# Where the block sums of x lie in SBUF: pads of 64 and 192 bytes around their low parts instead of 64 and 64

## The chip, the core and the metric

The kernel runs on one core of a Trainium2 chip. The metric is device time in microseconds from start to end of one execution, as a median of several runs.

## The reference

Two layers of a hybrid model on one sequence of 512 tokens with 1024 features, all in fp32. Each layer is a half-weighted SwiGLU feed-forward, a mixer (a gated linear recurrence with block attention in the first layer, a convolution branch with indexed attention in the second) and a second feed-forward:

```python
def swiglu(x, w_gate, w_up, w_down):
    return (jax.nn.silu(x @ w_gate) * (x @ w_up)) @ w_down

for i in range(DEPTH):                       # DEPTH = 2
    h = rms_norm(x, ffn1_norm[i])
    x = x + 0.5 * swiglu(h, ffn1_w_gate[i], ffn1_w_up[i], ffn1_w_down[i])   # 1024 -> 2816 -> 1024
    h = rms_norm(x, mix_norm[i])
    x = x + (even_mixer if i % 2 == 0 else odd_mixer)(h, ...)
    h = rms_norm(x, ffn2_norm[i])
    x = x + 0.5 * swiglu(h, ffn2_w_gate[i], ffn2_w_up[i], ffn2_w_down[i])
return x
```

## The kernel before

**Precision.** Every product is made of three fp32r matmuls: each operand is split into a high part (ScalarE, a copy that rounds) and a low part (VectorE, the value minus its high part), and high times high, high times low and low times high are added in PSUM. The three stand in `product` (lines 814 to 816, 512 columns in most uses) and in `gu_product` (lines 877 to 879, 256 columns). Each matmul loads its own 128x128 weights. In the profile's names, `ps_y<-xu_lo,gw_hi` is the matmul that streams `xu_lo` past the weights `gw_hi`: the moving operand stands first.

**The feed-forward.** There are four, each with 22 hidden tiles of 128 rows. The first two of each are plain: x (`xs_hi`, `xs_lo`) is streamed with 512 columns past gate and up weights. For the other twenty, 80 in all, gate and up are computed together by a scheme that saves one block product of eight: it needs sums of x's blocks and sums of weight blocks. Seven calls of `gu_product` make one tile, each with four triples, so 12 matmuls of 256 columns. Four calls stream blocks of x itself (`of_u`, from `xs_hi` and `xs_lo`), three stream the block sums (`of_xu`, from `xu_hi` and `xu_lo`). In a tile's steady order they are x, x, sums, x (the one left over from the tile before), sums, sums, x. After tiles 6, 14 and 22 come eight down units each, in which the hidden values `a_hi`, `a_lo` are streamed with 512 columns past `w_hi`, `w_lo`. All of this is issued in an order written out by hand; engines are tied by semaphores. Weights come by DMA into `raw` (down and mixer weights) and `gu` (gate and up weights), and ScalarE and VectorE split them into `w_hi`, `w_lo`, `gw_hi`, `gw_lo`. The block sums are written only at the start of each feed-forward: four ScalarE copies (line 1381) and four VectorE subtractions (line 1920).

**The mixers** use the same region of SBUF as the block sums for tiles of their own (`xc`, `isc`, `c_pad1` to `c_pad3`, `cv`, `ki`, `probs_more` and others), and the region of `gu`, `gw_hi`, `gw_lo` for q, k, v and the turned probabilities `pt`.

**Addresses.** `sb` gives each tile the next free bytes of a partition, rounded up to 32, from `top[0]`. `HALF_LINE` (64) is added to `top[0]` before and behind `xu_lo`. The first tile, `xu_hi`, lies at byte 1152. By the sizes of the tiles these are the offsets of their first bytes modulo 256; steps within the tiles that a matmul reads (blocks, pieces, halves of 256 columns) are multiples of 256, except in the convolutions, which stream `a` at steps of one element:

| tiles | before | after |
|---|---|---|
| `xu_hi` | 128 | 128 |
| `xu_lo` | 192 | 192 |
| mixers' tiles below the pads: `xc_hi`, `xc_lo` / `ki_hi`, `ki_lo`, `probs_more` | 128 / 0 | 128 / 0 |
| `xt`, `xs_hi`, `xs_lo`, `raw`, `w_hi`, `w_lo`, `a_hi`, `a_lo`, `scr` | 0 | 128 |
| `ident`, `ones` | 128 | 0 |
| `t0`, `t1`, `t2`, `diag`, `sqb`, `acc`, `rstd`, `half`, `bias_t` | 192 | 64 |
| `gu`, `gw_hi`, `gw_lo`; `q`, `k`, `v`, `pt`, `probs`, `bdr_hi` in the mixers | 64 | 192 |

And the distances, moving operand minus weights, modulo 256:

| pair | before | after |
|---|---|---|
| `xs_hi`, `xs_lo` past `gw_hi`, `gw_lo` | 192 | 192 |
| `xs`, `a` past `w`; `pt` past `v`; `k` past `q` | 0 | 0 |
| `xu_hi` past `gw_hi`, `gw_lo` | 64 | 192 |
| `xu_lo` past `gw_hi` | 128 | 0 |

```python
def gu_product(ps, piece, hi, lo, first, wait=None):
    for j in range(PAIRS):                   # 4
        ...
        pe.matmul(ps, gw_hi[:, piece, w], hi(j), ...)      # line 877
        pe.matmul(ps, gw_hi[:, piece, w], lo(j), ...)      # line 878
        mm = pe.matmul(ps, gw_lo[:, piece, w], hi(j), ...) # line 879
```

Of the kernel before, what the change touches and what calls it, by code (L numbers as in the profile page):

```python
# [49 lines left out]
SKEW = 640  # L50
COPIES = 32
HALF_LINE = 64

FFN_UNITS = len(GROUPS) * KT
PAIRS = KT // 2
# [137 lines left out]
def build(nc, xt_in, gu_stream, w_stream, vec_in, bd_in, relb_in, onehot_in, ident_in, out):  # L193
# [3 lines left out]
    with ExitStack() as ctx:  # L197
        top = [(nc.sbuf_base + 31) // 32 * 32]

        def sb(name, shape, dt=F32, at=None):  # L200

            size = int(np.prod(shape[1:])) * 4
            if at is None:
                at, top[0] = top[0], top[0] + (size + 31) // 32 * 32
            return nc.alloc_sbuf_tensor_at(name, shape, dt, offset=at)
# [6 lines left out]
        xu_hi = sb("xu_hi", [P, PAIRS, 3 * TH], F32R)  # L212
        top[0] += HALF_LINE
        xu_lo = sb("xu_lo", [P, PAIRS, 3 * TH], F32R)
        top[0] += HALF_LINE
        low_top = top[0]
        xt = sb("xt", [P, KT * T])
        xs_hi = sb("xs_hi", [P, KT, T], F32R)
# [2604 lines left out]
```

## Time and profile before

| | |
|---|---|
| median of 3 runs | 1905.33 us (1904.15 to 1905.38) |
| the profiled execution | 1904.64 us, its span 1902.8 us |
| granted TensorE clock over the span | 0.998 |
| TensorE busy | 1872.6 us (98%), 11916 matmuls |
| VectorE / ScalarE / GpSimd busy | 1458.7 / 1021.4 / 194.8 us |
| DMA moved | 271.66 MB, mean 143 GB/s |

A matmul's busy time in the groups is a latency with a modelled end, and neighbours overlap: the pace at which matmuls follow each other is the distance of their starts in the timeline, which prints them in hundredths of a microsecond. Twelve matmuls of 256 columns, one `gu_product`, are long enough to read a pace to 1 ns a matmul.

### The profile page before, as it was taken

What the parts mean: (1) busy time and instruction counts of PE and PEld (TensorE: products, weight loads), DVE (VectorE), ACT (ScalarE), POOL (GpSimd) and SP (SyncE); (2) the same over time, 40 slices, a digit from 0 to 9 for tenths busy, and PEclk for the clock granted to TensorE, in tenths of its full rate; (3) what the DMA queues carried; (4) which work ended last, traced back from release to release, by engine and by line L of the source; (5) the groups of instructions that cost most, each with busy time, mean ns of one, the idle gap of its engine ahead of it and who ended that gap; (6) DMA issues with size and microseconds to landing.
All of it is one profiled execution on the core that took longest, in us unless ns stands there. A gap on an engine that the chain in (4) does not pass through costs nothing.

```text
span 1902.8 us, 31445 instructions
## 1 busy us (share of the span) xinstructions
PE 1872.6 (98%) x11916; PEld 1668.0 (88%) x11916; DVE 1458.7 (77%) x2330; ACT 1021.4 (54%) x1640; POOL 194.8 (10%) x251
## 2 busy tenths in 40 slices
PE   7999999999999999999999999999999999999999
PEld 6899899888779899998889989887778789899997
DVE  8879587577679788597877859756989878687684
ACT  7546264477776355364645526455456766364451
POOL 1311010000001011010011101011111001011010
PEclk9999999999999999999999999999999999999999
DMA  7666662211137565563465546166765376565441
GB/s 241 155 200 183 174 167 64 100 67 67 56 111 183 167 169 146 150 173 109 134 170 156 152 143 179 45 165 161 167 153 131 86 200 170 158 183 161 133 112 67
DMA packets 94789, 271.66 MB, mean 143 GB/s; under 512 B 10504, under 2 KB 10760, under 8 KB 94640
## 3 DMA queue, kind: packets, MB, share of 16 engines
q1 hardware_dynamic: 63456, 201.22, 30.7%
q0 software_dynamic: 29232, 64.50, 19.3%
q10 hardware_dynamic: 1952, 3.93, 1.1%
q8 instruction: 95, 1.56, 0.3%
q14 instruction: 54, 0.44, 0.1%
HBM read 223.07 MB, written 2.77 MB: 119 GB/s over the span
## 4 chain that ended last, share of the span: by engine, by line
PE 88%; DVE 7%; ACT 3%; issue 2%; DMA 0%; DVEq 0%; ACTq 0%
PE ps_unit L814 13%; PE ps_unit L815 13%; PE ps_unit L816 13%; PE ps_y L878 6%; PE ps_y L877 6%; PE ps_y L879 6%; PE ps_s L877 4%; PE ps_s L878 4%; PE ps_t L878 4%; PE ps_t L877 4%; PE ps_t L879 4%; PE ps_s L879 4%; PE ps_s L814 1%; DVE cv L2479 1%; PE ps_s L815 1%
## 5 line engine op out<-in xcount | busy, mean ns | idle before, releaser
L1423 ACT ACTIVATE gw_hi<-gu 128x512 fp32r<-128x512 f32 (+1 forms) x400 | 319.0, 799 | 151.5 <-PE ps_s L879 69.3
L1954 DVE TENSOR_TENSOR gw_lo<-gu,gw_hi 128x512 fp32r<-128x512 f32 (+1 forms) x400 | 354.6, 901 | 46.5 <-ACT gw_hi L1423 35.0
L814 PE MATMUL ps_unit<-a_hi,w_hi 128*128 128x512 f32 x892 | 351.0, 394 | 5.4 <-DVE w_lo L1885 2.8
L815 PE MATMUL ps_unit<-a_lo,w_hi 128*128 128x512 f32 x892 | 348.0, 390 | 0.0
L816 PE MATMUL ps_unit<-a_hi,w_lo 128*128 128x512 f32 x845 | 329.2, 390 | 0.0
L1358 ACT ACTIVATE w_hi<-raw 128x1024 fp32r<-128x1024 f32 (+1 forms) x125 | 125.3, 1003 | 305.1 <-PE ps_unit L816 301.4
L814 PEld LDWEIGHTS ps_unit<-a_hi,w_hi 128*128 128x128 f32 x892 | 167.6, 188 | 44.3 <-DVE w_lo L1885 5.1
L2091 DVE TENSOR_TENSOR t<-ps_unit,half 128x512 f32<-128x512 f32 x96 | 66.4, 691 | 172.8 <-PE ps_unit L816 172.4
L815 PEld LDWEIGHTS ps_unit<-a_lo,w_hi 128*128 128x128 f32 x892 | 167.6, 188 | 32.8
L816 PEld LDWEIGHTS ps_unit<-a_hi,w_lo 128*128 128x128 f32 x845 | 158.6, 188 | 33.8
L879 PE MATMUL ps_y<-xu_hi,gw_lo 128*128 128x256 f32 x640 | 180.5, 282 | 0.0
L878 PE MATMUL ps_y<-xu_lo,gw_hi 128*128 128x256 f32 x640 | 179.2, 280 | 0.0
L877 PE MATMUL ps_y<-xu_hi,gw_hi 128*128 128x256 f32 x640 | 178.6, 279 | 0.0
L1885 DVE TENSOR_TENSOR w_lo<-raw,w_hi 128x1024 fp32r<-128x1024 f32 (+1 forms) x125 | 143.8, 1151 | 12.9 <-ACT w_hi L1358 12.9
L759 POOL DMA_DIRECT2D gu<-gu_stream_dram x80 | 74.8, 936 | 712.5 <-DMA gu<-gu_stream_dram 698.9
L814 PE MATMUL ps_unit<-xs_hi,w_hi 128*128 128x512 f32 x360 | 145.2, 403 | 0.0
L815 PE MATMUL ps_unit<-xs_lo,w_hi 128*128 128x512 f32 x360 | 140.6, 391 | 0.0
L877 PE MATMUL ps_s<-xs_hi,gw_hi 128*128 128x256 f32 x480 | 133.3, 278 | 0.0
L878 PE MATMUL ps_s<-xs_lo,gw_hi 128*128 128x256 f32 x480 | 133.3, 278 | 0.0
L878 PE MATMUL ps_t<-xs_lo,gw_hi 128*128 128x256 f32 x480 | 133.3, 278 | 0.0
L879 PE MATMUL ps_s<-xs_hi,gw_lo 128*128 128x256 f32 x480 | 133.2, 277 | 0.0
L877 PE MATMUL ps_t<-xs_hi,gw_hi 128*128 128x256 f32 x480 | 133.2, 277 | 0.0
(324 smaller groups left out, 4648.7 us busy)
## 6 DMA issues: line engine op xcount, KB each, us to landing
gu<-gu_stream_dram SPq DMA_DIRECT2D x176, 512.0 KB, 5.1
raw<-w_stream_dram SPq DMA_DIRECT2D x136, 512.0 KB, 3.3
gu<-gu_stream_dram SPq DMA_DIRECT2D x80, 256.0 KB, 3.0
gu<-gu_stream_dram POOLq DMA_DIRECT2D x80, 256.0 KB, 4.0
gu<-gu POOLq DMA_DIRECT2D x80, 256.0 KB, 3.3
w_lo<-raw POOLq DMA_DIRECT2D x28, 512.0 KB, 4.9
raw<-w_stream_dram SPq DMA_DIRECT2D x32, 384.0 KB, 3.5
w_lo_3rd<-raw POOLq DMA_DIRECT2D x15, 512.0 KB, 4.7
```

The lines of the kernel that those rows point to most:

```text
L759: pool.dma_start(gu[:, 8 + r, :], gu_stream[f, 1][:, 1, :], accum_op=ALU.add).then_inc(s1_landed, 16)
L814: pe.matmul(ps, lhs_hi, rhs_hi, start=first, stop=False)
L815: pe.matmul(ps, lhs_hi, rhs_lo, start=False, stop=False)
L816: return pe.matmul(ps, lhs_lo, rhs_hi, start=False, stop=last)
L877: pe.matmul(ps, gw_hi[:, piece, w], hi(j), start=first and j == 0, stop=False, skip_group_check=True)
L878: pe.matmul(ps, gw_hi[:, piece, w], lo(j), start=False, stop=False, skip_group_check=True)
L879: mm = pe.matmul(ps, gw_lo[:, piece, w], hi(j), start=False, stop=j == PAIRS - 1, skip_group_check=True)
L1358: act.activation(w_hi[:, s, 0:width(n)], raw[:, slot, 0:width(n)], ACT.Copy).then_inc(w_hi_done, 1)
L1423: act.activation(gw_hi[:, w, :], src, ACT.Copy).then_inc(gw_hi_done, 1)
L1885: dve.tensor_tensor(w_lo[:, s, w], raw[:, slot, w], w_hi[:, s, w].bitcast(F32), ALU.subtract).then_inc(w_lo_done, 1)
L1954: dve.tensor_tensor(gw_lo[:, w, :], src, gw_hi[:, w, :].bitcast(F32), ALU.subtract).then_inc(gw_lo_done, 1)
L2091: dve.tensor_tensor(t0[:, :], ps_unit[:, s, :], half[:, :], ALU.mult).then_inc(unit_read, 1)
```

## The change

One pad is 128 bytes longer. No instruction is added, removed or put elsewhere on any engine; the lines of the code move down by one.

```diff
 HALF_LINE = 64
+BANKS = 256
 ...
         xu_hi = sb("xu_hi", [P, PAIRS, 3 * TH], F32R)
         top[0] += HALF_LINE
         xu_lo = sb("xu_lo", [P, PAIRS, 3 * TH], F32R)
-        top[0] += HALF_LINE
+        top[0] += BANKS - HALF_LINE
         low_top = top[0]
         xt = sb("xt", [P, KT * T])
```

`xu_hi`, `xu_lo` and the mixers' tiles in that region stay at their bytes; every tile from `xt` on moves up by 128 bytes.

## Rows read from the trace of the kernel before

**Rows 1.** The page: TensorE's busy time; the chain that ended last, by engine.
```profile
PE 1872.6 (98%) x11916; PEld 1668.0 (88%) x11916; DVE 1458.7 (77%) x2330; ACT 1021.4 (54%) x1640; POOL 194.8 (10%) x251
...
PE 88%; DVE 7%; ACT 3%; issue 2%; DMA 0%; DVEq 0%; ACTq 0%
```
**Rows 2.** Groups by line and form, TensorE: count | busy us, mean ns of one.
```profile
L814 PE MATMUL ps_unit<-a_hi,w_hi 128*128 128x512 f32 x892 | 351.0, 394 | 5.4 <-DVE w_lo L1885 2.8 <-DVE a_lo L2539 0.9 <-DVE t L2156 0.9
...
L879 PE MATMUL ps_y<-xu_hi,gw_lo 128*128 128x256 f32 x640 | 180.5, 282 | 0.0
L878 PE MATMUL ps_y<-xu_lo,gw_hi 128*128 128x256 f32 x640 | 179.2, 280 | 0.0
L877 PE MATMUL ps_y<-xu_hi,gw_hi 128*128 128x256 f32 x640 | 178.6, 279 | 0.0
...
L877 PE MATMUL ps_y<-xs_hi,gw_hi 128*128 128x256 f32 x320 | 88.7, 277 | 0.0
L878 PE MATMUL ps_y<-xs_lo,gw_hi 128*128 128x256 f32 x320 | 88.6, 277 | 0.0
L879 PE MATMUL ps_y<-xs_hi,gw_lo 128*128 128x256 f32 x320 | 88.6, 277 | 0.0
```
**Rows 3.** Timeline, TensorE, first matmul of each gu_product: start us, latency us.
```profile
121.09 0.28 PE L877 MATMUL ps_t<-xs_hi,gw_hi 128*128 128x256 f32 x1
...
122.45 0.28 PE L877 MATMUL ps_y<-xu_hi,gw_hi 128*128 128x256 f32 x1
...
123.86 0.28 PE L877 MATMUL ps_s<-xs_hi,gw_hi 128*128 128x256 f32 x1
...
125.25 0.28 PE L877 MATMUL ps_y<-xu_hi,gw_hi 128*128 128x256 f32 x1
...
126.66 0.28 PE L877 MATMUL ps_t<-xu_hi,gw_hi 128*128 128x256 f32 x1
...
128.07 0.28 PE L877 MATMUL ps_t<-xs_hi,gw_hi 128*128 128x256 f32 x1
...
129.45 0.28 PE L877 MATMUL ps_y<-xs_hi,gw_hi 128*128 128x256 f32 x1
...
132.17 0.28 PE L877 MATMUL ps_y<-xu_hi,gw_hi 128*128 128x256 f32 x1
```
**Rows 4.** Busy times 112 to 188 us, eight hidden tiles: us (instructions), clock, DMA, GB/s.
```profile
112.00:188.00 76.00, 76.00 (x657) 75.96 (x656) 65.74 (x90) 46.12 (x77) 11.38 (x13) 1.00 0.65 176
```
**Rows 5.** Timeline: six down matmuls, then two products on x, then sums.
```profile
109.68 0.39 PE L816 MATMUL ps_unit<-a_hi,w_lo 128*128 128x512 f32 x1
...
111.04 0.39 PE L816 MATMUL ps_unit<-a_hi,w_lo 128*128 128x512 f32 x1
111.26 0.28 PE L877 MATMUL ps_y<-xs_hi,gw_hi 128*128 128x256 f32 x1
...
114.09 0.28 PE L877 MATMUL ps_y<-xu_hi,gw_hi 128*128 128x256 f32 x1
```
**Rows 6.** Timeline: a plain tile, from one matmul to the sixth after it.
```profile
31.23 0.39 PE L816 MATMUL ps_t<-xs_hi,gw_lo 128*128 128x512 f32 x1
...
32.63 0.39 PE L816 MATMUL ps_t<-xs_hi,gw_lo 128*128 128x512 f32 x1
```
**Rows 7.** Timeline: the attention's weighing, nine matmuls of 256 columns.
```profile
429.54 0.28 PE L814 MATMUL ps_y<-pt_hi,v_hi 128*128 128x256 f32 x1
...
430.61 0.22 PE L814 MATMUL ps_y<-pt_hi,v_hi 128*128 128x128 f32 x1
```
**Rows 8.** The page's DMA issues (median us to landing); ScalarE's group that awaits raw.
```profile
L1358 ACT ACTIVATE w_hi<-raw 128x1024 fp32r<-128x1024 f32 (+1 forms) x125 | 125.3, 1003 | 305.1 <-PE ps_unit L816 301.4 <-DMA raw<-w_stream_dram 3.5
...
gu<-gu_stream_dram SPq DMA_DIRECT2D x176, 512.0 KB, 5.1
raw<-w_stream_dram SPq DMA_DIRECT2D x136, 512.0 KB, 3.3
```

## The prediction

> **What bounds the kernel now.** I read the page first: its busy times and the chain that ended last. TensorE is busy for 1872.6 of 1902.8 us and 88% of the chain is TensorE's own work, so the end moves when matmuls start closer together or farther apart, and hardly for anything else [rows 1]. The change touches no instruction. It moves addresses, so the question is whether a matmul's pace depends on where its operands lie, and the trace can be asked that, because the kernel already has operands at several offsets. Two views answer it. The groups by line and form give one duration for each pair of operands: a 128x256 product that streams x (xs_hi, xs_lo) past the gate/up weights shows 276 to 278 ns, the same product that streams the block sums shows 279, 280 and 282 ns (xu_hi past gw_hi, xu_lo past gw_hi, xu_hi past gw_lo) [rows 2]. These are latencies with modelled ends, so what counts is the distance between starts, in the timeline. One hidden tile is seven gu_product calls of 12 matmuls, four on x and three on block sums. From 121.09 us on: x 1.36 us, sums 1.41, x 1.39, sums 1.41, sums 1.41, x 1.38, two on x 2.72, and the next tile's first sums start at 132.17, 9.72 us after 122.45 [rows 3]. So twelve matmuls on x take 1.36 us (113.3 ns each) when they stand far from sums, twelve on sums take 1.41 us (117.5 ns), and the x product right behind sums still pays 0.02 to 0.03 us. There is no gap: in the stretch of such tiles from 112 to 188 us TensorE is busy for all 76.00 us, VectorE for 65.74 and ScalarE for 46.12, at the full granted clock (1.00, which is 2.4 GHz) [rows 4]. A pace gained here is gained at the end.
>
> **What the offsets say.** The section on the kernel lists offsets modulo 256. Take the distance moving operand minus weights. x past gw: 192 (which is -64). w and a: 0. xu_hi past gw: 64. xu_lo past gw: 128. After the change x past gw stays 192 and w and a stay 0, since all of them move by 128 bytes together; xu_hi past gw becomes 192, that of x, and xu_lo past gw becomes 0, that of a past w. These are the two distances at which the trace has its best paces: 1.36 us for twelve 128x256 matmuls on x [rows 3], and 1.36 us for six 128x512 matmuls of the down projection, 109.68 to 111.04, again 113.3 ns for 256 columns [rows 5]. That speaks for the change. Three things in the trace speak against so simple a reading. First, distance 192 isn't always fast: the plain tiles stream x past gw with 512 columns and start 0.233 us apart (six in 1.40 us, 31.23 to 32.63) [rows 6]. Second, the same x products at the same distance run at the slow pace when they follow a down unit: two of them from 111.26 to 114.09 take 2.83 us, 1.41 for twelve, with nothing awaited [rows 5]. So a pace is a rhythm that the stream falls into, and the offset only decides which rhythms it may keep. Third, distance 0 with 256 columns stands in the attention (pt past v, both at 64): nine matmuls from 429.54 to 430.61 take 1.07 us, 118.9 ns each, if only in short bursts and with the columns in two pieces [rows 7].
>
> **The parts.** (1) xu_hi at x's distance: two of the three matmuls of a triple. Lower end 113.3 ns each as for x [rows 3], upper end 120 ns, about the attention's pace [rows 7]. I take 113.3, since the row is of the same loop, form and distance. (2) xu_lo at distance 0: between 113.3 ns (down units [rows 5]) and 118.9 ns (attention [rows 7]). I take 115, between them. One triple is then 113.3 + 115 + 113.3 = 341.6 ns, twelve matmuls 1.37 us instead of 1.41: 0.04 saved, three times a tile, 0.12 us. (3) The x products behind sums: if sums keep the even rhythm, there is nothing to recover from, 0.03 + 0.02 = 0.05 us a tile. Together 0.17 us a tile. There are 80 hidden tiles (640 ps_y matmuls on xu of each kind, two products of four a tile [rows 2]), so 13.6 us. If xu_lo too went at 113.3, the tile would save 3 x 0.05 + 0.05 = 0.20 us and the kernel 16.0; if each sum product saved only half, 3 x 0.025 + 0.02, about 0.09 us a tile, 7 us. (4) Everything else that moves does so by 128 bytes together with its partners: w, a, raw, x, gw, q, k, v, pt. I cost it at nothing; the pairs that do change their distance are xc past bdr, ki past the indexer's queries and some transposes of the mixers, fewer than 200 matmuls, at most some 10 ns each either way by the difference of 113 and 120, so within 2 us. (5) DMAs: raw goes from offset 0 to 128, gu from 64 to 192. 512 KB into raw land in 3.3 us, 512 KB into gu, which was never at a multiple of 256, in 5.1 [rows 8]. Even if raw took gu's time, 1.8 us more a load, only 3.5 us of all ScalarE waits were ended by raw's landing [rows 8], and DMA engines are 65% busy in the tiles [rows 4]; I take 0, with 2 us as the upper end. The Trainium skill, "DMA: Bandwidth & Descriptors", section "How a descriptor splits into AXI transactions", says that a transaction starts at a multiple of 256 bytes, so that a transfer of 4096 bytes a partition that starts at 128 needs one more piece than one at 0. No run here has shown it for raw; it would speak against this change, by the amounts just bounded.
>
> **Sum.** The profiled execution took 1904.64 us with a span of 1902.8; 1904.64 - 13.6 = 1891.0. The median of the three runs lies 0.7 us above that execution, so I say 1891.
>
> **Rivals.** *Nothing changes*, 1905. The pace of the sums may come from the step of 64 bytes between xu_hi and xu_lo, which stays, or repeat every 128 bytes, and then the move by 128 is no move: distances 64 and 128 before are the same as 192 and 0 after. For it: the rhythm of x after a down unit (1.41 us for twelve) has the very pace of the sums, as if 1.41 were simply what every stream takes that is out of step. Against: nothing; the trace holds no pair of matmuls that differ by 128 alone. The Trainium skill, "SBUF — State Buffer", section "Who interferes with whom", gives TensorE two independent read ports and says that it never waits on anyone; by that rule offsets would be indifferent, too. Here the trace disagrees with it as far as 279 to 282 ns stand against 277 for one form in one loop [rows 2], but it can't say which offsets are good.
> *The uneven rhythm is kept*, slower: before, the three sum products of a tile throw the stream out of the rhythm that a down unit left it in, and x settles to 1.36 behind them. At their new distances they may leave that rhythm as it is, and then all x products run at 1.41 us as in [rows 5]. A tile would pay 0.05 + 0.05 + 0.02 + 0.03 = 0.15 us more, 80 tiles 12 us: 1917. It decides as soon as the x products behind sums don't come back to 1.36.
> *The attention's pace*: sums at distance 0 and 192 go at 120 ns a matmul, 1.44 us for twelve, 0.03 more in 240 products: 7 us, 1912.
> *Half a gain*: one of the two kinds stays at its old pace, 1898.
>
> **Numbers.** The full gain has 0.30, the half 0.12, nothing changes 0.28, the uneven rhythm kept 0.20, the attention's pace 0.10. The likeliest is the full gain, barely; its own range is 1888 to 1895. A measurement of this kernel can tell about 0.2%, 3.8 us, from no change. Faster by more than that: 0.42; within it: 0.28; slower: 0.30. The range goes from 1888, where xu_lo too runs at 113.3 (16 us off the median is 1889), to 1917, the uneven rhythm kept; what is left out are mixtures of it with the costs in the mixers and of the DMAs.
>
> **What would show it.** If right: the three kinds of matmul on xu show 277 or 278 ns instead of 279, 280 and 282, twelve of them take 1.36 or 1.37 us in the timeline, the x product behind them 1.36, a tile 9.55 us instead of 9.72, and the down units stay at 227 ns a matmul. If nothing changes, the tile is 9.72 us again with the same three durations. If the uneven rhythm is kept, the sums show one even pace near 118 ns and x shows 1.41 us throughout. The prediction would also be wrong, by another way, if the down units left their 0.227 us: at the plain tiles' 0.233 the 892 triples on a [rows 2] alone would cost some 17 us. I give it no chance of its own, since their distance stays 0.

## The result, and the profile after

The changed kernel takes 1915.17 us (median of 4 runs, 1914.88 to 1916.05), the kernel before beside it 1904.74 us (1904.0 to 1905.38). The ratio is 1.0056, 95% interval 1.0041 to 1.0071: slower by 10.4 us, where 1891 us, a gain, was forecast. The span of the profiled execution grew from 1902.8 to 1913.0 us.

| | before | after |
|---|---|---|
| median | 1904.74 us | 1915.17 us |
| span, granted clock | 1902.8 us, 0.998 | 1913.0 us, 0.999 |
| TensorE busy | 1872.6 us | 1882.7 us |
| VectorE / ScalarE busy | 1458.7 / 1021.4 us | 1459.1 / 1021.2 us |
| distances between starts, summed over the trace: 3840 matmuls on x with 256 columns | 440.5 us | 450.4 us |
| the same: 2880 matmuls on sums | 339.2 us | 339.7 us |
| the same: 3791 matmuls of 512 columns past w | 885.2 us | 884.9 us |

The last three rows add, for every matmul of a kind, the time from its start to the next matmul's start. The sums of blocks, which the change moved, take what they took. Nearly all of the loss is in the products on x, whose distance to their weights did not change: 9.9 us.

These are the page's busy line and rows of the groups by line and form for TensorE (count, then busy us and mean ns of one). Line numbers are one higher than before.

```profile
PE 1882.7 (98%) x11916; PEld 1678.7 (88%) x11916; DVE 1459.1 (76%) x2330; ACT 1021.2 (53%) x1640; POOL 194.4 (10%) x251
...
L879 PE MATMUL ps_y<-xu_lo,gw_hi 128*128 128x256 f32 x640 | 180.3, 282 | 0.0
L878 PE MATMUL ps_y<-xu_hi,gw_hi 128*128 128x256 f32 x640 | 179.6, 281 | 0.0
L880 PE MATMUL ps_y<-xu_hi,gw_lo 128*128 128x256 f32 x640 | 178.9, 280 | 0.0
...
L878 PE MATMUL ps_y<-xs_hi,gw_hi 128*128 128x256 f32 x320 | 89.8, 281 | 0.0
L880 PE MATMUL ps_y<-xs_hi,gw_lo 128*128 128x256 f32 x320 | 89.7, 280 | 0.0
```

Against [rows 2] the matmuls on sums moved by 2 ns (from 279, 280 and 282 to 281, 282 and 280), and those on x went from 277 to 280 and 281. The timeline of the same tile as in [rows 3] and [rows 5], first matmul of each product of twelve, says where x pays. First the entry from a down unit, then a tile:

```profile
111.18 0.28 PE L878 MATMUL ps_y<-xs_hi,gw_hi 128*128 128x256 f32 x1
...
114.01 0.28 PE L878 MATMUL ps_y<-xu_hi,gw_hi 128*128 128x256 f32 x1
...
122.49 0.28 PE L878 MATMUL ps_y<-xu_hi,gw_hi 128*128 128x256 f32 x1
...
123.90 0.28 PE L878 MATMUL ps_s<-xs_hi,gw_hi 128*128 128x256 f32 x1
...
125.31 0.28 PE L878 MATMUL ps_y<-xu_hi,gw_hi 128*128 128x256 f32 x1
...
128.14 0.28 PE L878 MATMUL ps_t<-xs_hi,gw_hi 128*128 128x256 f32 x1
...
129.55 0.28 PE L878 MATMUL ps_y<-xs_hi,gw_hi 128*128 128x256 f32 x1
...
132.38 0.28 PE L878 MATMUL ps_y<-xu_hi,gw_hi 128*128 128x256 f32 x1
```

The two products at the entry take 2.83 us, as before. Then every product, on sums or on x, takes 1.41 us: there is no return to the 1.36 of [rows 3], and the tile lasts 132.38 - 122.49 = 9.89 us, seven times 1.413, instead of 9.72. It stays so until the stretch ends. Nothing waits: from 112 to 188 us TensorE is busy for 76.00 us as in [rows 4], with 648 matmuls instead of 657.

```profile
112.00:188.00 76.00, 76.00 (x648) 76.00 (x647) 64.66 (x88) 44.93 (x75) 11.41 (x13) 1.00 0.65 176
```

Where a stretch of hidden tiles is entered from plain tiles (in three feed-forwards of four), the changed kernel looks different. From 597 us on x takes 1.36 (1.37 to 1.38 right behind sums), sums take 1.42 to 1.44, and a tile 617.60 - 607.84 = 9.76 us:

```profile
607.84 0.28 PE L878 MATMUL ps_y<-xu_hi,gw_hi 128*128 128x256 f32 x1
...
609.27 0.29 PE L878 MATMUL ps_s<-xs_hi,gw_hi 128*128 128x256 f32 x1
...
610.64 0.28 PE L878 MATMUL ps_y<-xu_hi,gw_hi 128*128 128x256 f32 x1
...
617.60 0.28 PE L878 MATMUL ps_y<-xu_hi,gw_hi 128*128 128x256 f32 x1
```

So the stream of 256-column matmuls has two rhythms at the same operands and distances: an even one with 113.3 ns from start to start, and an uneven one with 117.8 ns on average (1413 ns for twelve). Theory A (A1 in the expectations below): a stretch keeps the rhythm with which it is entered unless some matmul in it throws the stream out. The kernel before came out of the down units unevenly, too, and its sums brought the stream back to the even rhythm; the change took that away.

### The profile page after: what moved, and what is told of

Same layout as the page of the kernel before. It is cut to its first block, busy times and chain, and to the rows that moved or that the text cites. A ratio compares the mean times of both kernels' runs of the same rounds, so it can differ in the third digit from the quotient of the medians.

```text
span 1913.0 us, 31445 instructions
## 1 busy us (share of the span) xinstructions
PE 1882.7 (98%) x11916; PEld 1678.7 (88%) x11916; DVE 1459.1 (76%) x2330; ACT 1021.2 (53%) x1640; POOL 194.4 (10%) x251
## 4 chain that ended last, share of the span: by engine, by line
PE 89%; DVE 6%; ACT 3%; issue 2%; DMA 0%; DVEq 0%; ACTq 0%
PE ps_unit L815 13%; PE ps_unit L816 13%; PE ps_unit L817 13%; PE ps_y L879 6%; PE ps_y L878 6%; PE ps_y L880 6%; PE ps_t L878 4%; PE ps_s L878 4%; PE ps_t L879 4%; PE ps_s L879 4%; PE ps_t L880 4%; PE ps_s L880 4%; PE ps_s L815 1%; PE ps_s L816 1%; PE ps_s L817 1%
## 5 line engine op out<-in xcount | busy, mean ns | idle before, releaser
L1886 DVE TENSOR_TENSOR w_lo<-raw,w_hi 128x1024 fp32r<-128x1024 f32 (+1 forms) x125 | 143.9, 1152 | 12.9 <-ACT w_hi L1359 12.9
L880 PE MATMUL ps_t<-xs_hi,gw_lo 128*128 128x256 f32 x480 | 134.6, 280 | 0.0
```

The costliest lines, as they stand in the source:

```text
L880: mm = pe.matmul(ps, gw_lo[:, piece, w], hi(j), start=False, stop=j == PAIRS - 1, skip_group_check=True)
L1886: dve.tensor_tensor(w_lo[:, s, w], raw[:, slot, w], w_hi[:, s, w].bitcast(F32), ALU.subtract).then_inc(w_lo_done, 1)
```

## The experiments

Every kernel here differs from the kernel before (or from the changed one, where said) in the few lines shown. "Distance" is moving operand minus weights modulo 256, as in the table of distances; high and low parts are those of the sums.

**The offset itself, or the distance?** 128 bytes are left free below everything, with the pads of before.

```diff
+        top[0] += 128
         low = top[0]
         xu_hi = sb("xu_hi", [P, PAIRS, 3 * TH], F32R)
```

> The pads are 64 and 64 as in the kernel before, but 128 bytes are left free below the block sums' high parts, so that every tile lies 128 bytes higher and every distance between a moving operand and its weights is that of before. Theory A (only distances between the two operands of a matmul count): the time of before, 1905 us, twelve matmuls on x at 1.36 us behind x and 1.38 behind sums, twelve on sums at 1.41. Rival B (the offset itself counts, of w, a, x or the gate/up weights, or of what the DMAs write): the changed kernel's time, 1915 us, with x at 1.41 us for twelve.

1904.7 us, ratio 1.0002 (0.9992 to 1.0011). The start distances sum to 440.5 us for x and 339.2 us for sums, what they were before. The offsets of w, a, x, the gate/up weights and the DMAs' targets are those of the changed kernel, so a move of all of them by 128 bytes has no part in the loss. What is left is the distances.

**Sums at x's own distance, high and low.**

```diff
         xu_hi = sb("xu_hi", [P, PAIRS, 3 * TH], F32R)
-        top[0] += HALF_LINE
         xu_lo = sb("xu_lo", [P, PAIRS, 3 * TH], F32R)
-        top[0] += HALF_LINE
```

> No pads: high and low parts of the sums lie at x's offset, distance 192 from the gate/up weights like x itself. Theory A1 (a stream keeps the rhythm with which it enters a stretch of hidden tiles, and only matmuls at another distance can throw it out of it): behind down units everything, x and sums, goes at 1.41 us for twelve, 1913 us in all; behind plain tiles everything at 1.36, the sums too. Theory A2 (distance 192 is good in itself, and it was the low part at distance 0 that spoilt the changed kernel): sums and x at 1.36 nearly everywhere, 1889 us.

1912.99 us, ratio 1.0043 (1.0028 to 1.0058), as A1 has it. With all distances equal the two rhythms stand side by side in one kernel. Its timeline behind plain tiles and, 70 us later, behind a down unit, first matmuls of products of twelve:

```profile
598.92 0.28 PE L877 MATMUL ps_y<-xu_hi,gw_hi 128*128 128x256 f32 x1
...
600.28 0.28 PE L877 MATMUL ps_s<-xu_hi,gw_hi 128*128 128x256 f32 x1
...
603.00 0.28 PE L877 MATMUL ps_s<-xs_hi,gw_hi 128*128 128x256 f32 x1
...
670.84 0.28 PE L877 MATMUL ps_y<-xu_hi,gw_hi 128*128 128x256 f32 x1
...
672.25 0.28 PE L877 MATMUL ps_s<-xs_hi,gw_hi 128*128 128x256 f32 x1
...
673.66 0.28 PE L877 MATMUL ps_y<-xu_hi,gw_hi 128*128 128x256 f32 x1
```

In the first stretch twelve matmuls take 1.36 us (4.08 us for the three products from 598.92 to 603.00), on sums as on x; in the second 1.41. Distance 192 is neither slow nor quick: it keeps what it is given.

**Modulo 256?** Pads 0 and 256 instead of none.

```diff
-        top[0] += HALF_LINE
         xu_lo = sb("xu_lo", [P, PAIRS, 3 * TH], F32R)
-        top[0] += HALF_LINE
+        top[0] += 256
```

> Pads 0 and 256: the distances of the kernel without pads, taken modulo 256, with 256 bytes more between the sums and all else. If the pattern repeats every 256 bytes, the paces and the time of the kernel without pads to within 1 us; if its period is longer, another time, anywhere from 1889 to 1917.

1913.43 us (1912.75 to 1913.57) against 1912.99 (1912.47 to 1913.29), with the same paces, and the same rhythm in every stretch but the first one, behind plain tiles at 37 us, which is even without pads and uneven here. 256 bytes between the sums and the rest change nothing else that can be measured; the change itself was 128 bytes.

**Which distance of the low parts?** First pads 128 and 128 (low parts at 64), then 192 and 64 (low parts at 128, as before). The high parts are at 192 in both, so the second is the half of the change that moves the high parts alone.

```diff
-        top[0] += HALF_LINE
+        top[0] += 192
         xu_lo = sb("xu_lo", [P, PAIRS, 3 * TH], F32R)
-        top[0] += HALF_LINE
+        top[0] += 64
```

> Pads 128 and 128: high parts at x's distance 192 as in the changed kernel, low parts at 64 instead of 0. Theory A1 (the high parts at x's distance leave the uneven rhythm as it is): 1913 to 1917 us, x at 1.41 for twelve behind down units. Rival C (one displaced matmul in three is enough to throw the stream out, but not at distance 0): x comes back to 1.36 to 1.38 behind sums, 1905 us or less.

1913.85 us, ratio 1.0048 (1.0033 to 1.0063): as the change, with x at 1.41 behind down units.

> Pads 192 and 64: high parts at distance 192 as in the changed kernel, low parts at 128 as in the kernel before. So this is the half of the change that moves the high parts alone. If the high parts decide (at x's distance the sums leave the uneven rhythm as it is, whatever the low parts do): 1913 to 1917 us, x at 1.41 for twelve behind down units and no return to 1.36. If the low parts at 128 are what throws the stream out: x back to 1.36 to 1.38, 1905 us or less.

1904.81 us, ratio 1.0002 (0.9992 to 1.0011), and with it my reading that the high parts decide fell. Its timeline, an entry behind a down unit and a tile:

```profile
111.16 0.28 PE L877 MATMUL ps_y<-xs_hi,gw_hi 128*128 128x256 f32 x1
...
113.99 0.28 PE L877 MATMUL ps_y<-xu_hi,gw_hi 128*128 128x256 f32 x1
...
122.36 0.28 PE L877 MATMUL ps_y<-xu_hi,gw_hi 128*128 128x256 f32 x1
...
123.79 0.28 PE L877 MATMUL ps_s<-xs_hi,gw_hi 128*128 128x256 f32 x1
...
125.15 0.28 PE L877 MATMUL ps_y<-xu_hi,gw_hi 128*128 128x256 f32 x1
...
132.08 0.28 PE L877 MATMUL ps_y<-xu_hi,gw_hi 128*128 128x256 f32 x1
```

The entry is uneven (2.83 us for two products), a product on sums takes 1.43, and the one on x behind it 1.36 at once. The tile is 9.72 us again: each product on sums costs 0.01 more than before, x behind sums 0.02 less. So with the high parts at 192, low parts at 128 throw the stream out, and low parts at 0, 64 or 192 don't. With the high parts where the change puts them, it is the move of the low parts from 128 to 0 that costs the 10 us. In these four kernels the step from the high to the low parts moves with the low parts' distance, and the runs don't tell the two apart; the step alone it can't be, since it is 64 both before and after the change. The other half alone (high parts at 64, low parts at 0) doesn't fit into a partition with pads, and was not tried; whether the low parts' move would cost the same there isn't shown.

**The entry as cause.** In the kernel without pads four extra triples stand ahead of the first product of each of the eight stretches that follow down units. They write to a PSUM bank that is idle then. In one kernel they stream x shifted by 32 and 48 elements, which puts them at distances 64 and 128; in its control unshifted, at 192.

```diff
+            def kick():
+                for _ in range(4):
+                    for w, x in ((gw_hi, xs_hi[:, 0, 32:288]), (gw_hi, xs_lo[:, 0, 48:304]), (gw_lo, xs_hi[:, 0, 32:288])):
+                        pe.matmul(ps_misc[:, 0:TH], w[:, 0, 0:P], x, start=True, stop=True)
 ...
                 pe.wait_ge(gw_lo_done, split_count(f, 0))
+                if (j - 1) in ENDS:
+                    kick()
```

> The kernel without pads, and at each of the 8 entries into hidden tiles behind a down unit 4 extra triples (12 matmuls of 256 columns, their result read by nobody) that stream x shifted by 32 and 48 elements, so at distances 64 and 128, those of the sums in the kernel before. Theory A1 (the entry decides the rhythm, and matmuls at these distances throw the stream out of the uneven one): the extra work costs 8 x 1.41 = 11 us, and the 448 products of these stretches go from 1.41 to 1.36, 24 us: 1900 us, with 1.36 for twelve on x and on sums alike. Rival D (something other than the entry makes the stretches behind down units slower, such as the loads or splits that run beside them): 1.41 as in the kernel without pads, 1924 us.

> The same 4 extra triples at the same 8 places, but not shifted, so at distance 192 like all matmuls around them. Theory A1: nothing throws the stream out, 1.41 us for twelve stays, and the extra work costs its 11 us: 1924 us. If extra triples at the entry, or the pause that they make for others, are what helps, whatever their distance: 1900 us as in the run with shifted ones.

Shifted: 1901.44 us, ratio 0.9983 (0.9974 to 0.9993). Unshifted: 1924.13 us, ratio 1.0105 (1.009 to 1.012). Both came within 1.5 us of what A1 gave. The two kernels run the same number of matmuls of the same form at the same places and differ by 22.7 us, by nothing but the addresses that 96 matmuls of 12,000 read. Rival D, that something beside TensorE slows these stretches whatever the entry, is out.

> One extra shifted triple instead of four at each of the 8 entries. It costs 8 x 0.35 = 3 us. If one triple is enough to throw the stream out of the uneven rhythm, 1913 + 3 - 24 = 1892 us; if it isn't, 1916.

1892.39 us, ratio 0.9939 (0.9925 to 0.9954): one triple is enough.

> The kernel without pads with a single extra matmul (x's high part shifted by 32 elements, distance 64) at each of the 8 entries. It costs 8 x 0.12 = 1 us. If one matmul is enough to throw the stream out of the uneven rhythm, 1913 + 1 - 24 = 1890 us; if not, 1914.

A single extra matmul, at distance 64: 1891.3 us, ratio 0.9931 (0.9914 to 0.9948). In its timeline the extra one (line 959) takes 0.12 us, and the product behind it is even at once:

```profile
113.05 0.28 PE L959 MATMUL ps_misc<-xs_hi,gw_hi 128*128 128x256 f32 x1
113.17 0.28 PE L877 MATMUL ps_y<-xs_hi,gw_hi 128*128 128x256 f32 x1
...
114.53 0.28 PE L877 MATMUL ps_s<-xs_hi,gw_hi 128*128 128x256 f32 x1
...
115.89 0.28 PE L877 MATMUL ps_y<-xu_hi,gw_hi 128*128 128x256 f32 x1
```

> The kernel without pads with one extra shifted triple at the 8 entries and at two more, the first hidden tiles of the first and the fourth feed-forward, which ran unevenly in the kernel with 8. Some 40 products more at 1.36 instead of 1.41 us, 2.1 us, for 0.7 us of triples: 1891 us.

A triple at ten places (of x's second tile instead of the first): 1891.77 us, ratio 0.9935 (0.992 to 0.995). All twelve stretches are now even. By the intervals it can't be told from the single matmul at eight places.

**What else switches the rhythm.** The traces show two things that theory A leaves out. In the one with one triple at eight places, the stretch from 1000 us on is even for some 45 products and then turns uneven, though every matmul in it stands at distance 192:

```profile
1058.63 0.28 PE L877 MATMUL ps_y<-xu_hi,gw_hi 128*128 128x256 f32 x1
...
1059.99 0.28 PE L877 MATMUL ps_t<-xs_hi,gw_hi 128*128 128x256 f32 x1
...
1061.35 0.29 PE L877 MATMUL ps_y<-xu_hi,gw_hi 128*128 128x256 f32 x1
1061.48 0.28 PE L878 MATMUL ps_y<-xu_lo,gw_hi 128*128 128x256 f32 x1
...
1062.77 0.28 PE L877 MATMUL ps_s<-xu_hi,gw_hi 128*128 128x256 f32 x1
```

Twelve matmuls take 1.36 us twice, then 1.42, and from there on 1.41. All that the trace shows at the turn are two starts that come 0.12 and 0.13 us behind the one before instead of 0.113. And at 38 us, in the first feed-forward, two starts come some 0.30 and 0.22 us behind the one before; in the kernel before and in both kernels with four triples the stream is even ahead of this pause and uneven behind it, while in the kernel with a single extra matmul it stays even behind a like pause. So a late start can take the even rhythm away, too. Nor do distances settle the entry from plain tiles: with the sums at distance 192 the second and third feed-forward enter evenly in every kernel, the fourth unevenly unless a triple stands there, and the first evenly in some kernels and unevenly in others.

**The changed kernel with one extra triple at the eight places.** Is the lost way out of the uneven rhythm the whole loss?

> The changed kernel (sums at distances 192 and 0) with the one extra shifted triple at each of the 8 entries behind down units. Theory A1: its whole loss is that its sums leave the uneven rhythm alone, so the extra triple brings the rest of each stretch to the paces that its own trace shows where it was entered from plain tiles: for twelve on x 1.36, on x behind sums 1.375, on sums 1.424 and 1.436, a tile 9.75 us instead of 9.89. 64 tiles save 9 us, the triples cost 3: 1909 us. If the low parts at distance 0 also end the even rhythm after a while, 1915 + 3 = 1918 us.

1910.24 us, ratio 1.0031 (1.002 to 1.0042). Its pace behind down units is now that of the changed kernel behind plain tiles, 132.17 - 122.42 = 9.75 us a tile:

```profile
122.42 0.28 PE L878 MATMUL ps_y<-xu_hi,gw_hi 128*128 128x256 f32 x1
...
132.17 0.28 PE L878 MATMUL ps_y<-xu_hi,gw_hi 128*128 128x256 f32 x1
```

So the rhythm is most of the loss, not all of it: beside the triples' 3 us some 0.03 us a tile stay, 2 us in 64 tiles, since sums at 192 and 0 cost more in the even rhythm than sums at 64 and 128 cost before (9.75 against 9.72 us), and the four tiles of the last feed-forward that stand behind plain tiles are still uneven, 0.7 us. These make up the 6.1 us over the kernel before to within the scatter of this kernel's runs (1908.64 to 1911.19).

**Everything at distance 0.** No pads, and 192 bytes ahead of the gate/up weights.

```diff
+        top[0] += 192
         stage = top[0]
         gu = sb("gu", [P, 11, PIECE])
```

> The kernel without pads, and 192 bytes left free ahead of the gate/up weights (and of the mixers' tiles in their place), so that x, sums and plain tiles all stand at distance 0 from them, like a and w. Theory A1: the stretches entered from down units, which run at distance 0 at their best pace, may keep it: 1.36 us for twelve and 0.227 us in the plain tiles, 1913 - 25 - 3 = 1885 us. Rival E (256 columns at distance 0 go at the attention's 119 to 120 ns): 1.43 to 1.44 us for twelve, 1913 + 11 = 1924 us.

1929.58 us, ratio 1.0133 (1.0116 to 1.015): rival E, and 6 us more than it gave. The timeline, six 512-column matmuls of a plain tile and one product of twelve:

```profile
31.43 0.39 PE L817 MATMUL ps_t<-xs_hi,gw_lo 128*128 128x512 f32 x1
...
32.79 0.39 PE L817 MATMUL ps_t<-xs_hi,gw_lo 128*128 128x512 f32 x1
...
116.21 0.28 PE L878 MATMUL ps_s<-xs_hi,gw_hi 128*128 128x256 f32 x1
...
117.65 0.28 PE L878 MATMUL ps_y<-xu_hi,gw_hi 128*128 128x256 f32 x1
```

Six of 512 columns take 1.36 us, where [rows 6] has 1.40 at distance 192; twelve of 256 columns take 1.44. Distance 0 is the better one for 512 columns and the worst seen for 256. The 6 us are my sum's fault. Against the kernel without pads the start distances grow by 19.3 us in the 256-column products (most went from 1.41 to 1.44, but those of twelve tiles from 1.36) and shrink by 2.3 in the plain tiles, 17.0 together, and the sum had put 11.

## Why the prediction was wrong

**What bounds the kernel** was right. TensorE's pace in the hidden tiles went straight into the end: 9.9 + 0.5 us of start distances, 10.4 us of time.

**Part (1), high parts at x's distance go at x's 113.3 ns**, is the step that failed, and (2) and (3) with it. It took 113.3 ns for a property of the distance. [rows 5] showed that it isn't, and the text said so one paragraph earlier: a pace is a rhythm, and offsets decide only which ones are kept. The sum then priced the block sums as if they stood in the even one. Behind down units the changed kernel never gets there, and where it is even, twelve matmuls on sums take 1.42 to 1.44 us, not 1.37: in company with high parts at 192, the low parts at 0 don't give the triple of 341.6 ns that **part (2)** put together, but one of 356 to 359.

**Part (3), x behind sums**, had the wrong sign: it was to gain 0.05 us a tile, and x lost 0.16 us a tile in the stretches behind down units (of the 0.17 between 9.89 and 9.72).

**Parts (4) and (5)**, that what moves together is free, and the DMAs too, were right: moving all by 128 bytes gave 1.0002. raw still lands in 3.3 us and the wait for it is still 3.5 us, as in [rows 8]. The rule of the Trainium skill on transfers that don't start at a multiple of 256 ("DMA: Bandwidth & Descriptors", "How a descriptor splits into AXI transactions") shows in neither number. After the change:

```profile
L1359 ACT ACTIVATE w_hi<-raw 128x1024 fp32r<-128x1024 f32 (+1 forms) x125 | 125.3, 1003 | 305.4 <-PE ps_unit L817 301.7 <-DMA raw<-w_stream_dram 3.5
...
raw<-w_stream_dram SPq DMA_DIRECT2D x136, 512.0 KB, 3.3
```

**The sum** has slips of 1 us at its ends, too: 1891.0 and the 0.7 us of the median are 1891.7, not 1891, and 16 us off the median is 1889, not the 1888 of the range. Neither bears on the outcome.

**The rivals.** *The uneven rhythm is kept* is what happened. 1917 us had been worked out for it and 1915.17 was measured, with the sign that had been named, x at 1.41 us throughout; it had been given a chance of 0.20. The price was 2 us high mainly because it counted all 80 tiles, while the stretches behind plain tiles are even in three feed-forwards. One part of its mechanism was wrong: it spoke of the sums' new distances together, and, with the high parts at 192, it is the low parts. *Nothing changes* fell with both its reasons, since a move by 128 bytes is a move, and the step of 64 bytes between high and low parts stayed while the rhythm did not. The prediction said that the trace holds no pair of matmuls that differ by 128 alone; xs_hi and xu_hi past gw_hi are nearly one, at 192 and 64 (277 and 279 ns in [rows 2]), if with different neighbours. *The attention's pace* was real for distance 0 throughout, but not for low parts alone. The rule of the Trainium skill, "SBUF — State Buffer", "Who interferes with whom", that TensorE with two independent read ports never waits on anyone, may hold between engines, which no run here tests; between the moving operand and the weights of its own stream, placement was worth 22.7 us here.

What should have been weighed more: the forecast needed the stream to leave the uneven rhythm, and the only thing that the trace had shown to take it out was the pair of distances that the change removed.

**A version that beats both.** The kernel without pads and with a single shifted matmul at eight entries takes 1891.3 us, 12.9 us less than the kernel before beside it (1904.17) and 24 less than the changed one. That the forecast said 1891 is chance: it counted on the even rhythm for the changed kernel, and this one, with other distances and eight extra matmuls, has it everywhere but in four tiles of the last feed-forward.

## What to carry to other kernels

Where TensorE is the bound and matmuls follow each other without gaps, read the distance between starts product by product and not only the mean: two clean values for one form at the same operands mean that the stream has rhythms, and then the entry into a loop is as much a thing to tune as the loop. Before an operand is moved, ask what it does for its neighbours: 2880 matmuls that looked slow by some 4 ns each were what kept most of the other 3840 quick. The test is cheap: one matmul with shifted columns ahead of the loop, and the same one unshifted as its control.

## What the runs showed of the hardware

- The pace of back-to-back fp32r matmuls that each load their own weights, at the full granted clock, depends on the distance of moving operand and weights: moving both by 128 bytes left the time (ratio 1.0002), and so did 256 bytes more between them (1912.99 and 1913.43 us). With 256 columns it was 113.3 or 117.8 ns at distance 192 and 120 at 0; with 512 columns 227 ns at 0 and 233 at 192.
- At distance 192 either pace lasted as long as a stretch does, 55 products of twelve in 75 to 78 us, with one exception in the traces: an even stretch turned uneven after some 45 products, at two starts that were 7 and 14 ns late. A single matmul at distance 64 behind a down unit turned 117.8 into 113.3 ns; four triples at 192 didn't.
- Inside a stretch, sums ended the uneven rhythm with high and low parts at 64 and 128; with high parts at 192 they ended it with low parts at 128, but not at 0, 64 or 192. Why one matmul at 64 does it at the entry when low parts at 64 don't do it inside, what sets the rhythm at an entry from plain tiles, and what in the chip holds it, stays open.
